# First two column blocks of an input projection: x read transposed, mean squares by a matmul with ones, token half 0 before half 1

## The chip, the cores and the metric

One core of a Trainium2 chip runs the whole kernel. The metric is the device time of one execution in microseconds (us), as the median of several runs. Engines are named as in the profile: PE is the matrix engine, DVE the vector engine, ACT the scalar engine, POOL the GpSimd engine, SP the engine that issues most of the DMAs.

## The reference, cut to what matters

The kernel computes one decoder layer in float32 on 1024 tokens of width 1024. Only its head matters here:

```python
def rms_norm(x, g):
    y = x * lax.rsqrt(jnp.mean(jnp.square(x), axis=-1, keepdims=True) + NORM_EPS)
    return y * g

h = rms_norm(x, in_norm_g)          # 1024 tokens x 1024 features
proj = h @ w_in                     # 1024 x 10240: q,k,v,g | xr,gr | m_ret,m_rnn
...
return rms_norm(x + ..., final_norm_g)
```

## The kernel before

**Products.** All products of the projection have features on the partitions: a weight tile of 128 features by 128 output columns is the stationary operand, and 512 tokens (a token half) move. So the normalised x has to lie with features on partitions, in `actv` (`ax(p, k, half)`: p is HI or LO, k one of 8 feature tiles, half one of 2 token halves). For accuracy each float32 operand is split in a rounded part HI and a rest LO, and each product is three matmuls, HI by HI, HI by LO and LO by HI (`mm3`, L322 to L326). The split is always the same pair of steps: ACT copies with rounding (HI), DVE subtracts (LO).

**The head of the program, lines L549 to L561, L936 to L945, L1319 to L1330, L1873 to L1882.** SP loads x as 8 tiles of 128 tokens by 1024 features (512 KB each), the first weight block (256 columns, slot 0 of `raw`) after the second tile, four small constants after the fourth, and the second weight block (slot 1) after the last. Per tile ACT squares it with a running sum along the free axis and takes the root (L349, L351); DVE takes the reciprocal of one number per partition and multiplies the tile (L356, L358). When four tiles are through, PE turns them by 32 transposes of 128x128 against an identity (L373), ACT copies each turned bank with the scale g to HI (L394), and DVE makes LO (L400). The second four tiles go the same way, their 32 transposes standing inside the product of slot 0 (`first_block`, L377).

**The order of the first two blocks.** `feature_jobs` runs, for one slot, four jobs: token half 0 with two column tiles, then token half 1 with two; slot 0 first, then slot 1. A job is 8 feature tiles by 3 matmuls, so the two blocks are 2 x 4 x 8 x 3 = 192 matmuls. Slot 0 uses PSUM banks 0 to 3, slot 1 banks 4 to 7. ACT applies the sigmoid from PSUM to `ost` (`evac_job`, L1339).

**What comes next.** The other 28 input blocks are done by a seven-product scheme with combined operands (`in_product`, L948). Its activation operands sc1 to sc4 are sums of quarters of the normalised x. In the kernel before these quarters are first put together again from HI and LO by `whole` (L1989, four calls: HI plus LO of 4 feature tiles), then combined (`comb`, L1994), and each result is split (`comb_hi` on ACT, L1369; `comb_lo` on DVE, L1997). The list of these DVE steps stands at L2004 to L2033, in one order with the preparation of the first weights (`combine_t13`, `combine_t2`, `combine_t4`, `prep_lo`). The first of the seven products (q == 0) waits for `prep_lo(0, 0, "b1")`, which in that list stands behind c3f, t13, the LO of sc3, t2, c2f, cbf and the LO of sc2. Engines run their instructions strictly in the order written; semaphores order them between engines, and every order is written out by hand.

**The rest** (the blocks' steady loop, retention, the recurrent unit, the output products, the convolution network) isn't touched but for counts of semaphores.

Of the kernel before, what the change touches and what calls it, by code (L numbers as in the profile page):

```python
# [14 lines left out]
F32 = mybir.dt.float32  # L15
# [93 lines left out]
def build(nc, a):  # L109
# [36 lines left out]
    x_in, _ = at("x_in", [P, KT, D], F32, B)  # L146
    xn_in, _ = at("xn_in", [P, KT, D], F32, B + 32 * K1)
# [30 lines left out]
    def chunk_set(tag, e):  # L178
# [70 lines left out]
    names = """alone const_in cs_in xt0 xt1 xt2 xt3 xt4 xt5 xt6 xt7 raw0 raw1 whi0 whi1 wsp0 wsp1 blk0 blk1 ini  # L249
        ss_done std_done rs_done xn_done tr_ps nhi_done nsp_done  # L250
# [6 lines left out]
        a11_in a12_in a22_in xs_hi xs_lo s3_f s2_f s1_f s4_f  # L257
        fraw0 fraw1 f_t13 f_t2 f_t4 f_hi f_lo f_pr f_u f_c tap0 tap1 conv_done g_silu a_mul h_st2
        dwr0 dwr1 dw_hi dw_lo dh_hi dh_lo d_b d_ps d_add tq_in tq_st tq_out
        out_t out_done""".split()  # L260
# [6 lines left out]
            "g_in": ("cs_in", 32), "d_s": ("rate", 3)}  # L267
# [92 lines left out]
    def turn_bank(n):  # L360

        return n if n < 8 else 4 + n % 4

    def turn_pe(pe, jobs, src, xn_sem, ps_sem, sp_sem):

        for n in jobs:
            half, k = n // 8, n % 8
            if k == 0:
                pe.wait_ge(xn_sem, 4 * half + 4)
            if n >= 8:  # L370
                pe.wait_ge(sp_sem, n - 3)
            for t in range(4):
                last = pe.transpose(ps[:, turn_bank(n), t * P:(t + 1) * P],  # L373
                                    src[:, 4 * half + t, k * P:(k + 1) * P], ident[:, :])
            last.then_inc(ps_sem, 1)

    def first_block(pe, slot_jobs, src_turn, sems):  # L377


        def around(job, k, after):  # L380
            if job == 0 and not after:
                pe.wait_ge(sems[2], k + 1)
            if job == 2 and k == 0 and not after:
                turn_pe(pe, range(8, 12), src_turn, *sems)
            if job == 2 and not after:
                pe.wait_ge(sems[2], 9 + k)
            if job == 2 and k < 4 and after:
                turn_pe(pe, (12 + k,), src_turn, *sems)
        slot_jobs(around)

    def turn_hi(act, n, dst, g, ps_sem, hi_sem):
        half, k = n // 8, n % 8
        act.wait_ge(ps_sem, n + 1)
        act.activation(dst(HI, k, half), ps[:, turn_bank(n), :], ACT.Copy,  # L394
                       scale=prm[:, g + k:g + k + 1]).then_inc(hi_sem, 1)

    def turn_lo(dve, n, dst, g, hi_sem, sp_sem):
        half, k = n // 8, n % 8
        dve.wait_ge(hi_sem, n + 1)
        dve.scalar_tensor_tensor(out=dst(LO, k, half), in0=ps[:, turn_bank(n), :], scalar=prm[:, g + k:g + k + 1],  # L400
                                 in1=dst(HI, k, half).bitcast(F32), op0=ALU.mult, op1=ALU.subtract).then_inc(sp_sem, 1)

# [6 lines left out]
    FIRST = [True, True, True, False, True, False, False]  # L409
    LAST = [False, True, True, False, False, True, True]  # L410
# [136 lines left out]
    with block:  # L547
# [3 lines left out]
        def _(sp_):  # L551
            x_t = a["x"].rearrange("b (t p) d -> p (b t) d", p=P)
            for t in range(KT):
                sp_.dma_start(x_in[:, t, :], x_t[:, t, :]).then_inc(sem[f"xt{t}"], 16)
                if t == 1:
                    load_columns(sp_, FIRST_PAIR, 0, a["w_in"][0], FIRST_COL)
                if t == 3:
                    for dst, src in ((prm, "prm"), (con, "con"), (ident, "ident"), (mask, "mask")):
                        sp_.dma_start(dst[:, :], a[src]).then_inc(sem["const_in"], 16)
# [2182 lines left out]
```

## Time and profile before

| what | before |
|---|---|
| median of 3 runs | 2028.03 us (2027.58 to 2028.80) |
| profiled execution, first to last instruction (span) | 2026.2 us |
| PE busy | 1987.1 us, 98% |
| DVE busy | 1404.8 us, 69% |
| ACT busy | 905.8 us, 45% |
| granted TensorE clock, mean | 0.999 |

The profile is of one execution; the profiled execution has no time of its own beside its span, so the 1.83 us between the span and the median stand for what lies around the span. "Busy" counts the time in which an engine has an instruction under way, and matmuls overlap: one takes some 0.39 us from start to end, but the next one starts 0.227 us after it.

### The profile page before, as it was taken

How to read it: one execution, taken by the hardware profiler on the slowest of the kernel's cores; microseconds unless marked ns; L12 is line 12 of the kernel's file. 1: busy time of each engine (PE TensorE's matmuls, PEld its weight loads, DVE VectorE, ACT ScalarE, POOL GpSimd, SP SyncE). 2: the span in 40 equal slices, each digit the busy share in tenths (PEclk: the TensorE clock that was granted, in tenths of full speed). 3: DMA queues.
4: the chain of work that ended last, by engine and by line, in shares of the span. 5: the costliest groups of instructions: out<-in, count | busy, mean ns of one | idle time of the engine just before them, and what ended most of it. 6: DMA issues, size and time to landing. Idle time of an engine off the chain costs nothing.

```text
span 2026.2 us, 25232 instructions
## 1 busy us (share of the span) xinstructions
PE 1987.1 (98%) x9332; PEld 1658.1 (82%) x9332; DVE 1404.8 (69%) x1714; ACT 905.8 (45%) x1154; POOL 228.9 (11%) x188
## 2 busy tenths in 40 slices
PE   7999999999999999999999999999999999999998
PEld 6888888888888888887788887898788888888887
DVE  6876876876744444614877877847988788776766
ACT  6443344344445555412444443345544444443335
POOL 0000000000000000001254544300000000000000
PEclk9999999999999999999999999999999999999999
DMA  5334445445444443445334234741222122156633
GB/s 203 125 132 138 154 161 182 154 159 185 164 169 175 156 156 125 146 150 187 99 120 120 78 119 131 264 147 52 94 83 104 62 83 104 62 172 232 209 101 133
DMA packets 184580, 283.01 MB, mean 140 GB/s; under 512 B 9792, under 2 KB 123840, under 8 KB 184256
## 3 DMA queue, kind: packets, MB, share of 16 engines
q1 hardware_dynamic: 164208, 204.52, 30.4%
q0 software_dynamic: 20304, 77.60, 9.8%
q8 instruction: 40, 0.66, 0.1%
q14 instruction: 28, 0.23, 0.0%
HBM read 198.20 MB, written 83.89 MB: 139 GB/s over the span
## 4 chain that ended last, share of the span: by engine, by line
PE 83%; DVE 11%; ACT 2%; issue 2%; DMA 1%; SPq 1%; DVEq 0%; ACTq 0%
PE ps L324 27%; PE ps L326 27%; PE ps L325 27%; DVE wx L1953 1%; DVE ws L307 1%; PE ps L1140 1%; DMA qkv<-scr_v 1%; DVE ost L1901 1%; DMA raw<-w_rnn_o 0%; PE ps L373 0%; DVE stage L2058 0%; ACT ri L1508 0%; DVE th L2142 0%; DVE ri L2153 0%; DVE th L2146 0%
## 5 line engine op out<-in xcount | busy, mean ns | idle before, releaser
L1366 ACT ACTIVATE wx<-raw 128x1024 fp32r<-128x1024 f32 (+1 forms) x152 | 137.4, 906 | 270.5 <-DVE raw L1929 148.3
L324 PE MATMUL ps<-xs,wx 128*128 128x512 f32 x612 | 239.0, 391 | 2.0 <-DVE xs L2381 1.6
L326 PE MATMUL ps<-xs,wx 128*128 128x512 f32 x612 | 238.2, 389 | 0.0
L325 PE MATMUL ps<-xs,wx 128*128 128x512 f32 x612 | 238.1, 389 | 0.0
L1953 DVE TENSOR_TENSOR wx<-raw,wx 128x1024 fp32r<-128x1024 f32 (+1 forms) x152 | 156.3, 1029 | 32.2 <-ACT wx L1366 32.2
L324 PE MATMUL ps<-sc,wx 128*128 128x512 f32 x448 | 174.8, 390 | 1.2 <-ACT ub L1398 1.2
L326 PE MATMUL ps<-sc,wx 128*128 128x512 f32 x448 | 174.3, 389 | 0.0
L325 PE MATMUL ps<-sc,wx 128*128 128x512 f32 x448 | 174.3, 389 | 0.0
L324 PEld LDWEIGHTS ps<-xs,wx 128*128 128x128 f32 x612 | 114.9, 188 | 28.6 <-issue 2.7
L326 PEld LDWEIGHTS ps<-xs,wx 128*128 128x128 f32 x612 | 114.9, 188 | 23.9
L325 PEld LDWEIGHTS ps<-xs,wx 128*128 128x128 f32 x612 | 114.9, 188 | 23.6
L1398 ACT ACTIVATE ub<-ps 128x512 f32<-128x512 f32 x112 | 66.4, 596 | 146.9 <-PE ps L326 144.4
L324 PE MATMUL ps<-actv,wx 128*128 128x512 f32 x336 | 130.7, 389 | 0.0
L325 PE MATMUL ps<-actv,wx 128*128 128x512 f32 x336 | 130.7, 389 | 0.0
L326 PE MATMUL ps<-actv,wx 128*128 128x512 f32 x336 | 130.7, 389 | 0.0
L307 DVE TENSOR_TENSOR ws<-raw,ws 128x2048 fp32r<-128x2048 f32 x32 | 73.3, 2289 | 78.6 <-ACT ws L303 78.6
L324 PE MATMUL ps<-wsd,hsd 128*128 128x512 f32 x308 | 119.9, 389 | 0.0
L325 PE MATMUL ps<-wsd,hsd 128*128 128x512 f32 x308 | 119.8, 389 | 0.0
L326 PE MATMUL ps<-wsd,hsd 128*128 128x512 f32 x308 | 119.8, 389 | 0.0
L303 ACT ACTIVATE ws<-raw 128x2048 fp32r<-128x2048 f32 x32 | 61.2, 1912 | 95.4 <-DMA raw<-w_rnn_o 52.2
L324 PE MATMUL ps<-yh,ws 128*128 128x512 f32 x256 | 100.1, 391 | 0.9 <-DVE yh L2239 0.8
L324 PEld LDWEIGHTS ps<-sc,wx 128*128 128x128 f32 x448 | 84.1, 188 | 20.2 <-ACT ub L1398 2.9
(270 smaller groups left out, 4826.8 us busy)
## 6 DMA issues: line engine op xcount, KB each, us to landing
raw<-w_in SPq DMA_DIRECT2D x80, 512.0 KB, 5.3
scr<-ost POOLq DMA_DIRECT2D x32, 1024.0 KB, 5.3
raw<-w_up SPq DMA_DIRECT2D x44, 512.0 KB, 3.9
tq<-w_down SPq DMA_DIRECT2D x88, 128.0 KB, 3.1
scr_t<-tq POOLq DMA_DIRECT2D x22, 512.0 KB, 3.2
scr_h<-vt POOLq DMA_DIRECT2D x11, 1024.0 KB, 4.3
scr_v<-ost POOLq DMA_DIRECT2D x8, 1024.0 KB, 4.4
qkv<-scr SPq DMA_DIRECT2D x64, 128.0 KB, 3.0
```

The lines of the kernel that those rows point to most:

```text
L303: act.activation(ws[:, slot, HI, 0:n], raw[:, slot, 0:n], ACT.Copy).then_inc(w_hi[slot], 1)
L307: dve.tensor_tensor(ws[:, slot, LO, 0:n], raw[:, slot, 0:n], ws[:, slot, HI, 0:n].bitcast(F32), ALU.subtract).then_inc(w_split[slot], 1)
L324: pe.matmul(out, w(HI), x(HI), start=first, stop=False, skip_group_check=True)
L325: pe.matmul(out, w(HI), x(LO), start=False, stop=False, skip_group_check=True)
L326: return pe.matmul(out, w(LO), x(HI), start=False, stop=last, skip_group_check=True)
L1140: last = pe.transpose(ps[:, 5, m * P:(m + 1) * P], on_of(h, j)[:, slot, m * P:(m + 1) * P], ident[:, :])
L1366: act.activation(dst, src, ACT.Copy).then_inc(sem["f_hi"], 1)
L1398: act.activation(ub[:, which, :], ps[:, 4 * u + BANKS[q], :], ACT.Copy).then_inc(sem["f_u"], 1)
L1901: ins = dve.scalar_tensor_tensor(out=dst, in0=s_, scalar=w, in1=dst, op0=ALU.mult, op1=ALU.add)
L1953: dve.tensor_tensor(dst, src, hi.bitcast(F32), ALU.subtract).then_inc(sem["f_lo"], 1)
```

## The change

The host passes x transposed as well (`xT`, features by tokens). The head loads `xT` instead of x, in 8 pieces of 2 feature tiles by 512 tokens (512 KB each): the four of token half 0, then the first weight block in two halves with semaphores of their own, the four constants, two pieces of half 1, the second weight block, and the last two pieces. There are no transposes. Per half: ACT squares four pieces, DVE adds the tiles pairwise (half 1: further, to one tile), PE multiplies a 128x128 matrix of ones by the sums of squares (plain float32, 512 columns; four matmuls for half 0, one for half 1), which gives the sum over all features of each token on every partition; ACT takes the root of that 128x512 tile, DVE its reciprocal. Then for each feature tile DVE multiplies x by g and by the reciprocal (`token_f`), ACT makes HI and DVE makes LO. The order of the 192 products is half 0 with slot 0, half 0 with slot 1, half 1 with slot 0, half 1 with slot 1. Because the normalised x stays in float32 in `xn_in`, the four calls of `whole` are dropped, and the counts of `q_st` change with them. Semaphores that are used only late in the program share those of the head (`late`).

```diff
@@ allocation
-    x_in, _ = at("x_in", [P, KT, D], F32, B)
-    xn_in, _ = at("xn_in", [P, KT, D], F32, B + 32 * K1)
+    x_in, _ = at("x_in", [P, 2, KT, HALF], F32, B)
+    xn_in, _ = at("xn_in", [P, 2, KT, HALF], F32, B + 32 * K1)
+    ones, e = at("ones", [P, P], F32, C + 16 * K1)
+    std_row, e = at("std_row", [P, 2, HALF], F32, e + 512)
+    rs_row, _ = at("rs_row", [P, 2, HALF], F32, e)
...
@@ SP
-            for t in range(KT):
-                sp_.dma_start(x_in[:, t, :], x_t[:, t, :]).then_inc(sem[f"xt{t}"], 16)
...
+            for n in range(4):
+                load_x(n)
...
+            sp_.dma_start(r[:, 0:4, :], v[:, 0:4, FIRST_COL:FIRST_COL + BC]).then_inc(sem["wa_in"], 16)
+            sp_.sem_inc(raw_in[0], 16)
+            sp_.dma_start(r[:, 4:8, :], v[:, 4:8, FIRST_COL:FIRST_COL + BC]).then_inc(raw_in[0], 16)
...
+            for n in range(4, 6):
+                load_x(n)
             load_columns(sp_, FIRST_PAIR, 1, w_in, FIRST_COL + BC)
+            for n in range(6, 8):
+                load_x(n)
@@ POOL
+            pool.memset(ones[:, :], 1.0).then_inc(sem["ini"], 1)
@@ PE
-            pe.wait_ge(sem["const_in"], 16 * 4)
-            in_sems = (sem["xn_done"], sem["tr_ps"], sem["nsp_done"])
-            turn_pe(pe, range(8), xn_in, *in_sems)
...
+            def square_sums(half, tiles, first_sum):
+                for n, k in enumerate(tiles):
+                    pe.wait_ge(sem["sq_p"], first_sum + n)
+                    h, at_ = xn_at(half, k)
+                    last = pe.matmul(ps[:, 7 - half, :], ones[:, :], xn_in[:, h, at_, :], start=n == 0,
+                                     stop=n == len(tiles) - 1, skip_group_check=True)
+                last.then_inc(sem["ss_ps"], 1)
+            square_sums(0, (0, 2, 4, 6), 1)
+            for half in range(2):
+                for slot in range(2):
+                    w = ws[:, slot, :, :].rearrange("p a (k c) -> p a k c", k=KT)
+                    for k in range(KT):
+                        if half == 0 and slot == 0 and k == 0:
+                            pe.wait_ge(sem["wa_lo"], 1)
+                        if half == 0 and k == (0 if slot else 4):
+                            block_ready(pe, FIRST_PAIR, slot)
+                        if half == 0 and slot == 1 and k == 3:
+                            square_sums(1, (0,), 8)
+                        if slot == 0:
+                            pe.wait_ge(sem["nsp_done"], 8 * half + k + 1)
+                        for m in range(2):
+                            last = mm3(pe, ps[:, 4 * slot + 2 * half + m, :], lambda q: w[:, q, k, m * P:(m + 1) * P],
+                                       lambda q: ax(q, k, half), k == 0, k == KT - 1)
@@ ACT
+            act.activation(rms_rs[:, 0:1], eps_norm, ACT.Sqrt)
...
+            for q in range(4):
+                squares(0, q)
+            act.wait_ge(sem["wa_in"], 16)
+            act.activation(ws[:, 0, HI, 0:BE // 2], raw[:, 0, 0:BE // 2], ACT.Copy).then_inc(sem["wa_hi"], 1)
+            deviations(0)
+            token_hi(0)
...
+            act.activation(ws[:, 0, HI, BE // 2:], raw[:, 0, BE // 2:], ACT.Copy).then_inc(w_hi[0], 1)
+            for n in range(1, 5):
+                token_hi(n)
+            split_hi(act, FIRST_PAIR, 1)
+            for n in range(5, 8):
+                token_hi(n)
+            for q in range(4):
+                squares(1, q)
+            deviations(1)
...
+            for n in range(8, 16):
+                token_hi(n)
+                if n in (11, 13):
+                    evac_job(FIRST_PAIR, 0, (n - 11) // 2, ACT.Sigmoid, 0)
@@ DVE
+            for q in range(4):
+                h, k = xn_at(0, 2 * q)
+                dve.wait_ge(sem["ss_done"], q + 1)
+                dve.tensor_tensor(xn_in[:, h, k, :], xn_in[:, h, k, :], xn_in[:, h, k + 1, :], ALU.add).then_inc(sem["sq_p"], 1)
+            dve.wait_ge(sem["wa_hi"], 1)
+            dve.tensor_tensor(ws[:, 0, LO, 0:BE // 2], raw[:, 0, 0:BE // 2], ws[:, 0, HI, 0:BE // 2].bitcast(F32),
+                              ALU.subtract).then_inc(sem["wa_lo"], 1)
+            def inverse(half):
+                dve.wait_ge(sem["std_done"], half + 1)
+                dve.reciprocal(rs_row[:, half, :], std_row[:, half, :]).then_inc(sem["rs_done"], 1)
+                dve.wait_ge(sem["rs_done"], half + 1)
...
+            inverse(0)
+            dve.wait_ge(sem["const_in"], 16 * 4)
+            for n in range(KT):
+                token_f(n)
+                if n:
+                    token_lo(n - 1)
+                if n == 1:
+                    dve.wait_ge(w_hi[0], 1)
+                    dve.tensor_tensor(ws[:, 0, LO, BE // 2:], raw[:, 0, BE // 2:], ws[:, 0, HI, BE // 2:].bitcast(F32),
+                                      ALU.subtract).then_inc(w_split[0], 1)
+            token_lo(KT - 1)
+            split_lo(dve, FIRST_PAIR, 1)
+            for n, (to, of, size, after) in enumerate(((0, 4, 2, 0), (2, 6, 2, 0), (0, 2, 2, 6), (0, 1, 1, 7))):
+                dve.wait_ge(sem["ss_done"], 8 if n else 7)
+                if after:
+                    dve.wait_ge(sem["sq_p"], after)
+                dve.tensor_tensor(xn_in[:, 1, to:to + size, :], xn_in[:, 1, to:to + size, :], xn_in[:, 1, of:of + size, :],
+                                  ALU.add).then_inc(sem["sq_p"], 1)
+            inverse(1)
+            for n in range(KT, 2 * KT):
+                token_f(n)
+                if n > KT:
+                    token_lo(n - 1)
+            token_lo(2 * KT - 1)
...
-            whole(caf, 0, 0)
-            whole(cbf, 0, 1)
-            step_done(2)
-            comb(c3f, caf, cbf, ALU.subtract)
+            comb(c3f, x11, x21, ALU.subtract)
             combine_t13(0, 0, (raw_in[0], IN_PAIRS[0] * 32 + 32))
+            comb_lo(sc3[:, LO, :, :], c3f, sc3[:, HI, :, :], 1)
+            combine_t2(0, 0, 0)
+            step_done(1)
+            comb(c2f, x22, c3f, ALU.subtract)
             step_done(3)
-            comb_lo(sc3[:, LO, :, :], c3f, sc3[:, HI, :, :], 1)
-            whole(cbf, 4, 1)
-            combine_t2(0, 0, 0)
-            step_done(5)
-            comb(c2f, cbf, c3f, ALU.subtract)
-            step_done(6)
-            comb(cbf, c2f, caf, ALU.add)
+            comb(cbf, x11, c2f, ALU.add)
             comb_lo(sc2[:, LO, :, :], c2f, sc2[:, HI, :, :], 2)
             prep_lo(0, 0, "b1", 1)
             combine_t4(0, 0, 0, 1)
-            step_done(8)
-            whole(caf, 4, 0)
+            comb(caf, x12, c2f, ALU.subtract)
```

## Rows read from the trace of the kernel before

**Rows 1.** The page's part 1, busy time of each engine and its share of the span.

```profile
PE 1987.1 (98%) x9332; PEld 1658.1 (82%) x9332; DVE 1404.8 (69%) x1714; ACT 905.8 (45%) x1154; POOL 228.9 (11%) x188
```

**Rows 2.** Waits of PE, whole run: us in total, times, longest; the two longest.

```profile
PE ps L373 <- DVE xn_in L358: 14.8, 1, 14.8
PE ps L324 <- DVE ktm L2268: 8.1, 11, 1.4
```

**Rows 3.** Timeline, PE, first 40 us: start, us, engine, line, operation, tiles.

```profile
14.76 5.82 PE L373 MATMUL ps<-ident,xn_in 128*128 128x128 f32 x32 [14.76 <-DVE xn_in L358]
20.34 0.47 PE L324 MATMUL ps<-actv,ws 128*128 128x512 f32 x1
...
31.33 1.91 PE L373 MATMUL ps<-ident,xn_in 128*128 128x128 f32 x16
...
33.49 0.50 PE L324 MATMUL ps<-actv,ws 128*128 128x512 f32 x1 [0.26 <-DVE actv L400]
```

**Rows 4.** Timeline, PE: the first of the seven products, and the fourth, 36 matmuls on.

```profile
68.10 0.39 PE L324 MATMUL ps<-actv,wx 128*128 128x512 f32 x1
...
76.26 0.39 PE L324 MATMUL ps<-sc,wx 128*128 128x512 f32 x1
```

**Rows 5.** Windows of the transposes: width, PE busy (count), PEld busy (count), granted clock, DMA.

```profile
14.70:19.20 4.50, 4.44 (x21) 4.47 (x22) 1.00 1.05 393
19.20:20.34 1.14, 1.14 (x13) 1.14 (x11) 1.00 1.09 384
```

**Rows 6.** Chain that ended last, first 20 us: start, us, what.

```profile
2.27 6.34 DMA raw<-w_in
```

**Rows 7.** Timeline, ACT: the first square, and the table load before the first sigmoid.

```profile
4.64 1.06 ACT L349 ACTIVATE xn_in<-x_in 128x1024 f32<-128x1024 f32 x1 [2.18 <-DMA x_in<-x]
...
39.05 1.28 ACT L1342 ACT_TABLE_LOAD   x1
```

**Rows 8.** Groups by line and form, DVE: reciprocals of 1 and 8 elements, a TENSOR_TENSOR of 8 elements.

```profile
L2218 DVE RECIPROCAL hn<-hn 128x1 f32<-128x1 f32 x32 | 4.9, 154 | 2.4 <-ACT hn L1559 2.4
L2117 DVE RECIPROCAL sp<-sp 128x8 f32<-128x8 f32 x1 | 0.2, 203 | 0.0
L2122 DVE TENSOR_TENSOR sp<-sp 128x8 f32<-128x8 f32 x7 | 1.2, 168 | 0.2
```

**Rows 9.** Timeline, DVE: the steps between the normalised x and the first of the seven products.

```profile
46.45 2.29 DVE L1995 TENSOR_TENSOR c3f<-caf,cbf 128x2048 f32<-128x2048 f32 x1
...
50.80 2.29 DVE L1999 TENSOR_TENSOR sc<-c3f,sc 128x2048 fp32r<-128x2048 f32 x1 [0.92 <-ACT sc L1371]
53.01 2.29 DVE L1991 TENSOR_TENSOR cbf<-actv 128x2048 f32<-128x2048 f32 x1
55.21 0.69 DVE L1922 TENSOR_TENSOR raw<-raw,tt 128x512 f32<-128x512 f32 x1
55.81 2.29 DVE L1995 TENSOR_TENSOR c2f<-cbf,c3f 128x2048 f32<-128x2048 f32 x1
...
62.55 1.22 DVE L1953 TENSOR_TENSOR wx<-raw,wx 128x1024 fp32r<-128x1024 f32 x1
63.87 0.69 DVE L1929 TENSOR_TENSOR raw<-raw 128x512 f32<-128x512 f32 x1
```

**Rows 10.** Timeline, DVE: four SCALAR_TENSOR_TENSOR of 512 elements in a row.

```profile
32.69 2.73 DVE L400 SCALAR_TENSOR_TENSOR actv<-ps,prm,actv 128x512 fp32r<-128x512 f32 x4 [4.51 <-ACT actv L394]
```

**Rows 11.** Groups by line and form, ACT: rounding copies of 512 from SBUF and PSUM.

```profile
L1577 ACT ACTIVATE yh<-ych 128x512 fp32r<-128x512 f32 x32 | 20.2, 632 | 20.1 <-DVE ych L2232 20.1
L394 ACT ACTIVATE actv<-ps,prm 128x512 fp32r<-128x512 f32 x16 | 10.4, 689 | 8.1 <-PE ps L373 8.0
```

**Rows 12.** Timeline, DVE: LO of b22, and the first long idle time after them.

```profile
76.57 0.68 DVE L1953 TENSOR_TENSOR wx<-raw,wx 128x512 fp32r<-128x512 f32 x1
...
85.25 0.69 DVE L2058 TENSOR_TENSOR stage<-ub 128x512 f32<-128x512 f32 x1 [2.06 <-ACT ub L1398]
```

**Rows 13.** DMA issues of the first 60 us: KB each, median us to landing.

```profile
scr_a<-actv SPq DMA_DIRECT2D x1, 2048.0 KB, 9.8
```

More of the change, by code:

```diff
@@ L358, in norm_apply_dve @@
         dve.tensor_scalar(dst[:, t, :], src[:, t, :], rms_rs[:, t:t + 1], None, ALU.mult).then_inc(xn_sem, 1)
[L360 to L401, printed above, removed]
     E_B11, E_B21, E_T4, E_T2, E_B22, E_T1, E_T3 = range(7)
@@ L936, in _ @@
                 pe.sem_inc(blk[slot], 1)
[L937 to L945 removed]
+            pe.wait_ge(sem["ini"], 2)
+            def square_sums(half, tiles, first_sum):
[21 more added lines that the diff above has]
+                                       lambda q: ax(q, k, half), k == 0, k == KT - 1)
+                            if k == KT - 1:
+                                last.then_inc(blk[slot] if half == 1 and m == 1 else sem["job"], 1)
             def in_product(b, q, u):
@@ L1328, in _, with squares, deviations @@
-            split_hi(act, 0, 1)
-            for n in range(8, 16):
-                turn_hi(act, n, ax, PRM["in_g"], sem["tr_ps"], sem["nhi_done"])
+            act.activation(rms_rs[:, 0:1], eps_norm, ACT.Sqrt)
+            def squares(half, q):
+                act.wait_ge(sem[f"xt{4 * half + q}"], 16)
+                h, k = xn_at(half, 2 * q)
+                act.activation(xn_in[:, h, k:k + 2, :], x_in[:, half, 2 * q:2 * q + 2, :], ACT.Square).then_inc(sem["ss_done"], 1)
+            def deviations(half):
+                act.wait_ge(sem["ss_ps"], half + 1)
+                act.activation(std_row[:, half, :], ps[:, 7 - half, :], ACT.Sqrt, scale=1.0 / D,
+                               bias=eps_norm).then_inc(sem["std_done"], 1)
@@ new lines, in token_hi @@
+            def token_hi(n):
+                half, k = n // KT, n % KT
+                h, at_ = xn_at(half, k)
+                act.wait_ge(sem["xn_done"], n + 1)
+                act.activation(ax(HI, k, half), xn_in[:, h, at_, :], ACT.Copy).then_inc(sem["nhi_done"], 1)
+            for q in range(4):
[3 more added lines that the diff above has]
+            deviations(0)
@@ L1340, in evac_job @@
                 half, m = job // 2, job % 2
-                job_wait(i, slot, job)
+                if i == FIRST_PAIR and job < 3:
+                    act.wait_ge(sem["job"], FIRST_JOBS.index((slot, job)) + (0 if (slot, job) == (1, 2) else 1))
+                else:
+                    job_wait(i, slot, job)
                 act.activation(ost[:, slot, m, half * HALF:(half + 1) * HALF], ps[:, 4 * slot + job, :],
@@ L1380, in _ @@
             prep_hi(0, 0, "b1")
-            for job in range(2):
-                evac_job(FIRST_PAIR, 1, job, ACT.Sigmoid, 0)
             act.wait_ge(sem["f_t4"], 1)
@@ L1385, in _ @@
             prep_hi(0, 0, "t2")
-            comb_hi(sc1[:, HI, :, :], cbf, 7)
-            evac_job(FIRST_PAIR, 1, 2, ACT.Sigmoid, 0)
-            evac_job(FIRST_PAIR, 1, 3, ACT.Sigmoid, 0)
+            comb_hi(sc1[:, HI, :, :], cbf, 4)
+            for job in range(2, 4):
+                evac_job(FIRST_PAIR, 1, job, ACT.Sigmoid, 0)
             act.wait_ge(blk[1], IN_PAIRS[0] + 1)
@@ new lines, in _, with token_f @@
+            dve.wait_ge(sem["wa_hi"], 1)
[5 more added lines that the diff above has]
+                dve.wait_ge(sem["rs_done"], half + 1)
+            def token_f(n):
+                half, k = n // KT, n % KT
+                h, at_ = xn_at(half, k)
+                dve.scalar_tensor_tensor(out=xn_in[:, h, at_, :], in0=x_in[:, half, k, :],
+                                         scalar=prm[:, PRM["in_g"] + k:PRM["in_g"] + k + 1], in1=rs_row[:, half, :],
+                                         op0=ALU.mult, op1=ALU.mult).then_inc(sem["xn_done"], 1)
```

134 lines of the change are left out of this document (61 added, 73 removed).

## The prediction

> **What bounds the kernel now.** I read the page's busy times first: PE is busy 98% of the span, the other engines far less [rows 1]. So time can come only from what PE waits for and from what PE does beside products. The list of PE's waits says where it waits: 14.8 us before the first transpose, then 8.1 us in eleven pieces in a later stage that the change doesn't touch [rows 2]. The timeline of the opening shows the rest [rows 3]: transposes from 14.76, the first product at 20.34, and between 31.33 and the end of the two blocks a second set of transposes with a short wait at 33.49. The first of the seven products starts at 68.10 [rows 4]. The 192 products of the two blocks need 192 x 0.2267 = 43.5 us, the pitch being (76.26 - 68.10)/36 [rows 4]; 68.10 - 20.34 = 47.8, so 4.2 us between them is transposes and waiting. Everything after 68.10 hangs on PE, so the change is worth what it moves the start of the first of the seven products. I call that moment Q.
>
> **Part 1, the start for half 0.** ACT's first square starts when the first 512 KB are there, 4.64 [rows 7]; the fourth piece of 512 KB had landed at 2.27 + 6.34 = 8.61 [rows 6]. I take the same times for pieces of xT (2 KB rows between the 4 KB rows of x and the 1 KB rows of w_in, which that row covers), so the fifth piece, the weights, lands near 9.9, before its turn. The squares end at 5.7 and at 9.7; DVE adds in 0.69 [rows 9]. (On DVE the next instruction starts some 0.09 before the last one's end: 0.60 apart for 512 elements, 1.13 for 1024, 2.20 for 2048, and 0.66 for a SCALAR_TENSOR_TENSOR of 512, (2.73 - 0.75)/3 [rows 9, 10].)
>
> The plain float32 matmul with ones isn't in the trace. Below: one pass, 0.23. Above: `mm3` computes three of the four HI/LO combinations in three pitches, the fourth makes 4 x 0.2267 = 0.91. I take 0.91, since the f32 transposes, which only pass a value on, already take more than their share: 128 columns in 1.14/11 = 0.10 against 0.057 for a quarter of 0.2267 [rows 5]. The Trainium skill (FP8 and Floating Point Precision, TensorE Precision Notes) gives four passes for true FP32, the same sum; no row here shows such a matmul.
>
> Pace: the first 21 transposes, after 14.7 us of idleness, came 0.214 us apart, the next ones 0.10 [rows 5]. The granted clock stands at 1.00 in both rows, yet the ratio is that of 1.2 to 2.4 GHz and lasts 4.4 us. So I cost PE at half pace for its first 4.4 us. Sums start at 6.5, 8.3, 10.1 and, with the pace rising at 10.9, 11.4; the last ends at 12.3, with drain 12.4. The root from PSUM takes 0.69 [rows 11]: 13.1.
>
> **The reciprocal** is the term that decides. One of 512 elements isn't there. One element takes 154 ns, eight take 203; an ordinary operation of eight takes 168 [rows 8]. Slope: 49/7 = 7.0 ns an element; or (203 - 168)/7 = 5.0 more than the ordinary one's 1.07 (2.20/2048 from [rows 9]), that is 6.1. I take 6.4, nearer the second, which compares equal sizes: 0.15 + 511 x 0.0064 = 3.4 us. Ends: 0.69, as any 512 elements, if eight elements say nothing of many, and 4.4 above (see the third rival).
>
> It ends at 16.6. Then token_f 0.75, ACT's HI 0.63, token_f of the next tile beside it, LO 0.69 [rows 9, 10, 11]: first product at **18.8** instead of 20.34, though 32 transposes are gone. PE has been idle for over 6 us, so half pace again: six products 2.6, to 21.4. DVE puts the second half of the weights' LO (1.13) between: LO of tile 1 comes at 21.5. Tile 1 runs slow until 23.2, ends at 23.7; six more tiles at 1.36 make 31.9, faster than DVE's 0.66 + 0.60 = 1.26 a tile needs PE to wait for. Slot 1 follows: its split ends near 31.5, its raw load landed long before. 48 x 0.2267 + 0.91 for the sum of half 1: 43.7. Half 1 is 96 x 0.2267 = 21.8: PE would be ready for Q at **65.5**, 2.6 us earlier than before, by PE's own work.
>
> **Part 2, DVE's list for half 1.** The sum stands at slot 1's fourth tile, 31.9 + 4.1 = 36.0. The four adds (3 x 1.13 + 0.69, behind the split that ends at 31.5) end at 35.8, just in time. Sum to 37.1, root 37.8, reciprocal 41.2, token_f to 42.0. Then seventeen steps in turn, 0.66 + 8 x 1.26: last LO at 52.0, and 0.4 for ACT, which has a table load of 1.28 [rows 7] and two sigmoids between tiles 11 and 14: 52.4. Now the old list runs: before, from the start of c3f to the end of b1's LO was 63.77 - 46.45 = 17.3, of which 2.2 was a `whole` [rows 9], so 15.1. Q = **67.6**. The chain on DVE is 2.1 longer than PE's own; PE waits at Q for b1's LO.
>
> So `whole` saves four times 2.2 us of DVE, three of them ahead of Q, and PE is rid of the 4.2 us of half 1's transposes and wait, but the two reciprocals put 6.8 us back on the one chain, and half 1's float32 work (16 steps) stands behind the second.
>
> **What is free, and its cover.** Scratch store of a quarter of half 1 (wait for 12 LOs): issued near 49 instead of 43, 9.8 to land [rows 13]: 59, needed after 65. The sigmoids' stores through POOL's queue leave up to 15 us later, their buffers are next written some 20 us on. The constants land some 2 us later, needed at 16.6. The memset of ones lies under the loads. SP issues the same 16 DMAs. After Q: LO of t4 comes about 3.1 us after Q, used at Q + 5.4; b22 at about Q + 11, used at Q + 16.3. LO of b22 began at 76.57 before [rows 12] and begins near 78.2 now; DVE was idle 2.06 us before 85.25 [rows 12], which takes that up. The 64 transposes and 5 sums otherwise leave no trace. So I carry the shift of Q to the end unchanged.
>
> **Sum.** 67.6 - 68.10 = -0.5 us against a span of 2026.2, 2025.7; the median stands 1.83 above the span: **2027.5 us**. Measurement tells 0.2%, 4.1 us, from no change.
>
> **Rivals.**
> 1. *The reciprocal is an ordinary operation* (0.69). Both terms lose 2.8. Then the chain is at 67.6 - 5.5 = 62.1, PE's own work at 65.5 - 2.8 = 62.7 decides: -5.4, 2022.6. For it: nothing wide was seen. Against: eight elements cost more than an ordinary eight. 0.12.
> 2. *The sums are one pass each* (0.23). The last ends 1.2 earlier, the second sum 0.7: 65.7, 2025.6. 0.10.
> 3. *DVE's chain costs more than it saves*: the reciprocal takes eight elementary steps an element. 8 x 1.07 x 512 = 4.4 us, twice 1.0 more: Q at 69.6, PE waiting 3 us for b1's LO, 2029.5, slower. From 3.7 us a reciprocal on, Q passes 68.10; only from 5.7 us would it be over 0.2%. Against: the slopes of 6.1 to 7.0. The Trainium skill (VectorE: DVE Perf Modes, First, the fixed hardware budget) describes the reciprocal as an iterative divide with a repeat count of 8, which would be this case; no wide reciprocal is in the trace of before. 0.14.
>
> The forecast has what is left, 0.64.
>
> Range: forecast's own 2025.5 to 2028.7 (reciprocal 3.2 to 3.7, sums 0.23 to 0.91, loads 0.5 us either way, 0.6 of run spread); with rivals 2 and 3 it is 2024.2 to 2029.8; rival 1 stays outside. Faster by over 0.2%: 0.13; within: 0.84; slower: 0.03 (a reciprocal near 6 us, or a late load on top).
>
> **What would show it.** RECIPROCAL of 128x512 near 3.4 us, twice, PE idle during the first; first product near 18.8, with the first pitches near 0.43; PE waiting some 2 us at the first `actv,wx` product, released by b1's LO on DVE, near 67.6; no later wait of PE that wasn't there. Wrong if that product starts before 64 or after 70, if PE waits within half 1, or if waits grow later while Q moved early.

## The result, and the profile after

| what | before | after |
|---|---|---|
| median | 2027.85 us (2026.91 to 2029.49, 20 runs) | 2030.59 us (2028.94 to 2033.33, 20 runs) |
| ratio | | 1.0014, 95% interval 1.0008 to 1.0020 |
| profiled execution, span | 2026.2 us | 2029.0 us |
| PE busy | 1987.1 us | 1988.1 us |

The change costs 2.7 us, a loss of 0.14%: smaller than the 0.2% that the prediction called the least to be told, yet outside its range. First the totals of the changed kernel and the list of what PE waits for, to be read beside [rows 1, 2].

```profile
PE 1988.1 (98%) x9278; PEld 1652.2 (81%) x9278; DVE 1410.4 (70%) x1721; ACT 902.2 (44%) x1141; POOL 225.5 (11%) x189
```

```profile
PE ps L332 <- DVE ktm L2328: 8.1, 11, 1.4
PE ps L921 <- DVE xn_in L1906: 6.7, 1, 6.7
PE ps L332 <- DVE actv L1930: 6.4, 1, 6.4
...
PE ps L332 <- DVE wx L2025: 1.9, 1, 1.9
PE ps L332 <- ACT ub L1427: 1.8, 4, 0.8
...
PE ps L332 <- DVE yacc L2312: 1.3, 1, 1.3
PE ps L332 <- DVE ws L315: 1.3, 1, 1.3
...
PE ps L332 <- DVE mix L2393: 0.6, 1, 0.6
```

The 14.8 us before the first transpose have become 6.7 and 6.4, before and behind the sums of squares, with PE's 6.67 us for the sums between them. Two entries are as foreseen: the wait at `wx` (Q, the start of the first of the seven products) and the one at `actv`. Three are not: 0.8 us at once for ACT's `ub` (before, no wait for it was over 0.3), and, in a stage 1200 us behind the change, 1.3 us for `yacc` and 1.3 us for DVE's split of the weights of `w_out` (`ws`). One wait of that stage has shrunk, `mix` from 1.7 to 0.6. The timeline gives the places; PE first.

```profile
6.65 6.67 PE L921 MATMUL ps<-xn_in,ones 128*128 128x512 f32 x8 [6.65 <-DVE xn_in L1906]
19.75 0.77 PE L332 MATMUL ps<-actv,ws 128*128 128x512 f32 x1 [6.43 <-DVE actv L1930]
20.31 0.63 PE L333 MATMUL ps<-actv,ws 128*128 128x512 f32 x1
20.74 0.63 PE L334 MATMUL ps<-actv,ws 128*128 128x512 f32 x1
...
66.19 0.39 PE L334 MATMUL ps<-actv,ws 128*128 128x512 f32 x1
68.45 0.47 PE L332 MATMUL ps<-actv,wx 128*128 128x512 f32 x1 [1.87 <-DVE wx L2025]
...
84.63 0.39 PE L334 MATMUL ps<-sc,wx 128*128 128x512 f32 x1
85.85 0.47 PE L332 MATMUL ps<-sc,wx 128*128 128x512 f32 x1 [0.83 <-ACT ub L1427]
```

The sums end at 13.3, the first product starts at 19.75 with matmuls 0.43 apart, the blocks end at 66.42 (the last start and one pitch) and Q is at 68.45, 0.35 later than in [rows 4]. At 85.85, where the seventh of the seven products begins, PE has lost another 1.0 us: the pitch before it is 1.22 instead of 0.227. Nothing like it is in the trace of before. Now DVE and ACT around these places.

```profile
14.07 3.35 DVE L1914 RECIPROCAL rs_row<-std_row 128x512 f32<-128x512 f32 x1 [0.81 <-ACT std_row L1327]
...
38.62 3.35 DVE L1914 RECIPROCAL rs_row<-std_row 128x512 f32<-128x512 f32 x1 [1.94 <-ACT std_row L1327]
...
64.88 2.28 DVE L2066 TENSOR_TENSOR sc<-c2f,sc 128x2048 fp32r<-128x2048 f32 x1
67.08 1.22 DVE L2025 TENSOR_TENSOR wx<-raw,wx 128x1024 fp32r<-128x1024 f32 x1
...
82.55 1.22 DVE L2025 TENSOR_TENSOR wx<-raw,wx 128x1024 fp32r<-128x1024 f32 x1
83.87 0.69 DVE L2001 TENSOR_TENSOR raw<-raw 128x512 f32<-128x512 f32 x1
```

```profile
84.59 0.63 ACT L1392 ACTIVATE wx<-raw 128x512 fp32r<-128x512 f32 x1 [4.38 <-DVE raw L2001]
85.13 1.06 ACT L1427 ACTIVATE ub<-ps 128x512 f32<-128x512 f32 x2
```

Both reciprocals take 3.35 us, and b1's LO (67.08) ends just before Q: the chain of the prediction. The second place is read backwards from PE's 85.85. The product there was released by ACT's copy `ub` at 85.13. That copy needs only PSUM, but ACT had been idle for 4.38 us, standing in its order at the HI copy of block 1's t4, which waits for DVE's t4 (L2001), started at 83.87. So DVE's list, which the prediction left at Q, decides PE's time once more, 17 us later.

Six profiles show how much of this is the kernel's and how much the execution's: of the unchanged kernel, beside the one shown, two more (and one with an unused input, below), of the changed one three in all.

| | first product | Q | shift at 100 us | span |
|---|---|---|---|---|
| before, 3 profiles | 20.34, 19.92, 21.20 | 68.10, 67.67, 68.94 | 0, -0.43, +0.81 | 2026.2, 2026.1, 2026.8 |
| after, 3 profiles | 19.75, 19.51, 18.94 | 68.45, 68.21, 68.34 | +1.30, +1.03, +1.92 | 2029.0, 2028.7, 2029.4 |

(The shift is that of PE's same matmul against the first profile of before.) On the average Q is 0.1 later, PE's matmuls near 100 us are 1.3 later, and the end is 2.7 later. The third profile after is of experiment 12, whose computation and order are those of the changed kernel.

### The profile page after: what moved, and what is told of

Read it like the earlier page. It is cut to its first block, busy times and chain, and to the rows that moved or that the text cites. A ratio compares the mean times of both kernels' runs of the same rounds, so it can differ in the third digit from the quotient of the medians.

```text
span 2029.0 us, 25120 instructions
## 1 busy us (share of the span) xinstructions
PE 1988.1 (98%) x9278; PEld 1652.2 (81%) x9278; DVE 1410.4 (70%) x1721; ACT 902.2 (44%) x1141; POOL 225.5 (11%) x189
## 4 chain that ended last, share of the span: by engine, by line
PE 78%; DVE 13%; issue 4%; ACT 3%; POOL 1%; DMA 1%; SPq 0%; DVEq 0%; POOLq 0%; ACTq 0%
PE ps L332 26%; PE ps L334 25%; PE ps L333 25%; DVE wx L2025 1%; DVE ws L315 1%; POOL msg L894 1%; PE ps L1137 1%; DVE ost L1975 1%; DMA qkv<-scr_v 0%; DVE tt L1987 0%; PE ps L921 0%; DVE stage L2118 0%; ACT ri L1537 0%; DVE th L2202 0%; DVE ri L2213 0%
## 5 line engine op out<-in xcount | busy, mean ns | idle before, releaser
L315 DVE TENSOR_TENSOR ws<-raw,ws 128x2048 fp32r<-128x2048 f32 x31 | 72.0, 2324 | 78.0 <-ACT ws L311 78.0
```

What stands on the lines that cost most here:

```text
L315: dve.tensor_tensor(ws[:, slot, LO, 0:n], raw[:, slot, 0:n], ws[:, slot, HI, 0:n].bitcast(F32), ALU.subtract).then_inc(w_split[slot], 1)
```

## The experiments

Differences are of medians, to the kernel before on the same chip, whose median there was 2028.82 (experiments 1 to 4), 2028.23 (5 to 8), 2028.29 (9, 10), 2028.37 (11) and 2027.88 us (12). Each interval is some 1.8 us to either side, so differences of 1 us are read from the profiles and only supported by the medians. A wait of PE is given as the time lost against its pitch of 0.227; the idle time in the profile's rows is some 0.16 shorter.

The theories: the loss is DVE's list, bound until some 100 us, through the wait at Q and the one at the seventh product; or it is the one wait at Q; or PE's clock, which a long wait lets fall; or something late and unconnected.

**1. b1's LO earlier.** DVE's `prep_lo` of b1 goes up to stand right behind the LO of sc3. On ACT (not shown) b1's HI goes up too, and the HI of sc2 goes behind two sigmoids.

```diff
             comb_lo(sc3[:, LO, :, :], c3f, sc3[:, HI, :, :], 1)
+            prep_lo(0, 0, "b1", 1)
             combine_t2(0, 0, 0)
...
             comb_lo(sc2[:, LO, :, :], c2f, sc2[:, HI, :, :], 2)
-            prep_lo(0, 0, "b1", 1)
```

> Only the place of the first weights' split is changed: on ACT and DVE the HI and LO of b1 stand right behind those of sc3, ahead of c2f, cbf and the split of sc2. Nothing is left out. Theory A (DVE's list is the bound, in two places: at the first of the seven products by b1's LO, and again before the seventh by the U copy that ACT makes only after DVE's t4 of block 1): the first of the seven products starts near 66.4 instead of 68.45, when PE's own work is done, but t4's LO then holds the third product by about 0.4, and the seventh product still starts near 85.8, because DVE's list is as long as before; total within 0.3 us of the changed kernel. Rival B (the wait at the first product is the loss and the rest is independent of it): the seventh product starts 2.0 earlier and the kernel is 2.0 us faster than the changed one.

2030.91 us, +2.1 (ratio 1.0011, 1.0002 to 1.0020). The wait at Q is gone, Q at 66.19:

```profile
65.97 0.39 PE L334 MATMUL ps<-actv,ws 128*128 128x512 f32 x1
66.19 0.39 PE L332 MATMUL ps<-actv,wx 128*128 128x512 f32 x1
```

and the list of PE's waits has it at the other place, longer:

```profile
PE ps L332 <- ACT ub L1427: 3.0, 4, 2.1
```

Two us gained at Q, of which 1.3 were lost again before the seventh product (the expectation had all of it lost). So the wait at Q alone is not the cause; DVE's list behind it is.

**2. The copy ahead of the wait.** ACT copies the first block's sixth partial result out of PSUM before it waits for block 1's t4.

```diff
+                        in_copy(b, u, U_P5)
...
-                in_copy(b, u, U_P5)
+                if b:
+                    in_copy(b, u, U_P5)
```

> Only ACT's order in the first of the seven-product blocks is changed: the copy of the fifth product (U_P5) stands ahead of the wait for DVE's t4 of block 1. Nothing is left out. Theory A: the wait of 1.0 us before the seventh product goes, its start moves from 85.85 to about 84.85, the first product stays at 68.45; 1.0 us faster than the changed kernel. Rival B (the wait was for something else, the split of b22 or the fourth operand on DVE): the seventh product stays at 85.85.

2031.24 us, +2.4 (1.0011, 1.0002 to 1.0020). No wait at the seventh product, and no gain. This profile alone doesn't show that the edit removed the wait, since PE was itself late here; 1 against 3 does. PE at Q, and its windows there (width, PE busy, granted clock, DMA share, GB/s):

```profile
68.26 0.66 PE L332 MATMUL ps<-actv,wx 128*128 128x512 f32 x1 [1.87 <-DVE wx L2027]
68.72 0.63 PE L333 MATMUL ps<-actv,wx 128*128 128x512 f32 x1
69.15 0.63 PE L334 MATMUL ps<-actv,wx 128*128 128x512 f32 x1
```

```profile
68.26:71.71 3.45, 3.45 (x9) 0.52 0.99 330
71.71:76.00 4.29, 4.29 (x20) 0.99 0.26 106
```

Behind the same wait of 2.0 us the granted clock stood at 0.52, that is 1.2 GHz, and eight matmuls came 0.427 apart instead of 0.227: 1.6 us. In the profile shown after, the same stretch was at full pace. So the wait at Q has a second price, which only some executions pay.

**3. Both edits of 1 and 2.**

> Both edits of e1_b1_first and e2_copy_first. Theory A: first product near 66.4, seventh near 83.2, 2.6 us faster than the changed kernel, so together they are worth more than the 0 and the 1.0 of each alone. Rival B (the two waits add): 3.0 us. If the late part of the loss (about 1.4 us that the profile shows between 1282 and 1302 us in the changed kernel) comes from the change, it is in this kernel too, and the kernel is about level with the one before; if it is the spread of one execution, this kernel is 1.2 us faster than the one before.

2029.52 us, +0.7 (1.0005, 0.9996 to 1.0014), 2.0 to 2.5 us faster than the changed kernel (whose own differences are +2.7 in the first result and +3.2 in 5) where 2.6 were expected. Block 0's seventh product, which waited 2.1 us in 1, waits no more. The wait has moved on by one block, to block 1's seventh product:

```profile
99.54 0.39 PE L334 MATMUL ps<-sc,wx 128*128 128x512 f32 x1
101.67 0.50 PE L332 MATMUL ps<-sc,wx 128*128 128x512 f32 x1 [1.74 <-ACT ub L1427]
```

**4. Without the cost of both reciprocals.** The inverse of the root is left out: the normalised x of the two blocks and the operands is multiplied by the root itself.

```diff
-                dve.reciprocal(rs_row[:, half, :], std_row[:, half, :])
+                dve.tensor_scalar(rs_row[:, half, :], std_row[:, half, :], 1.0, None, ALU.mult)
```

> The two reciprocals of 512 elements are replaced by multiplications by 1.0, so x is scaled by the deviation and not by its inverse; the rest is the changed kernel. Theory A (each reciprocal is about 2.8 longer than an ordinary operation, the first delays PE's start, the second DVE's list): first product of the two blocks near 17.0 instead of 19.75, the first of the seven near 63.7 (PE's own work), no wait before the seventh, 5.8 us faster than the changed kernel. Rival B (only the first reciprocal is on the path, because the wait at the seven products has another cause): a rigid shift of 2.8 us with both later waits left, 2.8 us faster.

2023.99 us, -4.8 (0.9977, 0.9968 to 0.9986). First product 16.02, Q 63.18 with no wait, no long wait at the seventh product. At 100 us it is 6.1 us ahead of the changed kernel; the instruction that took the reciprocal's place takes 0.43, so 2 x 2.92 = 5.8 us were taken out. All of both reciprocals lies on the path. By the medians the kernel is 7.5 to 8.0 us faster than the changed one; the 2 us beyond 5.8 are within what two intervals of 1.8 allow, and part of them can be the clock at Q, which this kernel doesn't pay.

**5. The changed kernel again**, as a mate for 6 to 8.

> The changed kernel once more, unaltered, for a second profile. Theory C (the wait of 2.0 us at the first of the seven products lets PE's clock fall in some executions, so that they lose up to 1.7 us more): either a profile like the first, with 0.227 us between matmuls behind that wait, or one with 0.427 for the next eight, as in the profile of e2_copy_first. Theory D (the 1.4 us lost between 1282 and 1302 us in the first profile come from the change): the loss is there again. If D is wrong it is anywhere between 0 and 1.5, as it was in the four other kernels (0.0 to 1.1).

2031.46 us, +3.2 (1.0014, 1.0005 to 1.0023). Waits as after: 2.0 at Q, 1.0 at the seventh product, 1.1 near 1300 us.

**6. The wait at Q filled** with eight matmuls whose result nobody uses; Q itself doesn't move.

```diff
+            pe.wait_ge(sem["evac"], 1)
+            for n in range(8):
+                pe.matmul(ps[:, 0, :], ax(HI, n, 0, slice(0, P)), ax(HI, n, 0), start=True, stop=True, skip_group_check=True)
```

> Eight extra matmuls (1.8 us) are put on PE between the two blocks and the first of the seven products, into a bank that is overwritten right after, so that PE works through most of its wait for b1's LO. Theory C: the first of the seven products stays near 68.4 and the wait before it shrinks to 0.2; its clock can't fall there, and the median over the executions comes down from that of the changed kernel by 0.3 to 1.0 us (1.7 times the share of the executions in which it fell). Rival (the fall of the clock has no part in the median): the same median as a1_again. If PE, and not DVE, were the bound at that point, the kernel would be 1.8 us slower.

2029.64 us, +1.4 (1.0008, 0.9999 to 1.0017). PE does 1.97 us of useless work:

```profile
66.01 1.97 PE L986 MATMUL ps<-actv 128*128 128x512 f32 x8
68.04 0.47 PE L332 MATMUL ps<-actv,wx 128*128 128x512 f32 x1
```

Q is at 68.04 against 68.21 and the seventh product still waits, yet the median is 1.8 (the mean 1.2) below that of 5. That is more than expected (0.3 to 1.0), within the intervals' reach, and the two profiled executions don't show it (spans 2029.0 and 2028.7). What the rows show is 1.6 us in the two executions whose clock fell (here in 2, and in 12), two of the five profiles with this wait: an estimate of 0.6 us on the average. That it is more is not shown.

**7 and 8. One reciprocal each**, replaced as in 4 (the inverse is left out for token half 1, then for half 0).

> Only the second reciprocal is replaced by a multiplication by 1.0 (token half 1 is scaled by the deviation, not its inverse); the first stays. Theory A: PE starts at 19.5 as before, DVE's list is 2.8 shorter: first of the seven products at PE's own 66.3, no wait left before the seventh (f_t4 of block 1 comes at 81.8), 3.0 us faster than a1_again. Rival B (only the first reciprocal counts): no change.

> Only the first reciprocal is replaced (token half 0). Theory A: everything on PE and on DVE's list moves 2.8 us earlier, PE starts at 16.8, and both waits stay as they are, 2.0 and 1.0; 2.8 us faster than a1_again. With r2_norec_half1 that makes the 5.8 of r1_norec_both. Rival (the start of PE isn't on the path, since DVE's list is the bound): half of the gain or less.

2027.05 us, -1.2 (0.9994, 0.9985 to 1.0003), and 2028.08 us, -0.15 (0.9998, 0.9989 to 1.0007), 4.4 and 3.4 us below 5. At 100 us the profiles are 3.4 and 3.1 us ahead of that of 5, where 2.9 were taken out (0.6 of the 3.4 is that PE started and finished the two blocks earlier in that execution): each reciprocal is paid in full. Without the first, everything moves as a block, and both waits stay (2.0 and 0.95). Without the second, DVE's list is ahead of PE, and there is no wait at Q (65.61) and 0.3 at the seventh product.

**9. A narrow reciprocal.** The sums go to tokens on partitions, 128x4; root and reciprocal are taken there, and four transposes of a broadcast column spread the result over all partitions, in PSUM.

```diff
-                    last = pe.matmul(ps[:, 7 - half, :], ones[:, :], xn_in[:, h, at_, :], start=n == 0,
+                    for c in range(4):
+                        last = pe.matmul(ps[:, 7, c:c + 1], xn_in[:, h, at_, c * P:(c + 1) * P], ones[:, 0:1],
...
+                for c in range(4):
+                    last = pe.transpose(ps[:, 6, c * P:(c + 1) * P],
+                                        rs_row[:, half, c:c + 1].to_broadcast([P, P]), ident[:, :])
...
-                dve.reciprocal(rs_row[:, half, :], std_row[:, half, :])
+                dve.reciprocal(rs_row[:, half, 0:4], std_row[:, half, 0:4])
```

> The mean squares of a half are taken with the tokens on the partitions: per chunk of 128 tokens a matmul with the squares as stationary operand and one column of ones moving, so that root and reciprocal are of 128x4 and not of 128x512; then four f32 transposes of the reciprocal, repeated along the free axis, against the identity put it on all partitions in PSUM, where token_f reads it. Nothing is left out. Theory A (the wide reciprocals cost it): PE's first product near 17.1 instead of 19.5, first of the seven near 64.2, no wait before the seventh; some 5 us faster than the changed kernel, 2 to 3 faster than the one before. Rival (the small f32 matmuls cost what the reciprocal did, since each loads 128 columns of stationary operand four times at the slow pace): first product not before 18.5 and at most 2 us faster than the changed kernel.

2026.45 us, -1.8 (0.9992, 0.9983 to 1.0001), 4.6 to 5.1 us faster than the changed kernel, as expected. First product 17.89 and Q 65.00, each some 0.8 later than expected, no wait at Q.

**10. The same with both edits of 1 and 2.**

> f1_spread with the two edits of e3_both. Theory A: PE is the bound at the first seven products already in f1, so that the order is worth at most 0.3 to 0.8 us more here (the waits before the seventh products of the first two blocks).

2025.19 us, -3.1 (0.9985, 0.9976 to 0.9994): the lowest median of the kernels that compute the whole layer, and the only one of them that is faster than the kernel before by more than its interval. It is 1.3 us below 9 (0.3 to 0.8 expected), which is within the intervals. PE, DVE and ACT at the head of its profile:

```profile
6.71 6.96 PE L922 MATMUL ps<-ones,xn_in 128*128 128x1 f32 x32 [6.71 <-DVE xn_in L1921]
14.24 1.11 PE L931 MATMUL ps<-ident,rs_row 128*128 128x128 f32 x4 [0.57 <-DVE rs_row L1929]
17.68 0.76 PE L332 MATMUL ps<-actv,ws 128*128 128x512 f32 x1 [2.32 <-DVE actv L1945]
```

```profile
14.00 0.18 DVE L1929 RECIPROCAL rs_row<-std_row 128x4 f32<-128x4 f32 x1 [1.02 <-ACT std_row L1340]
```

```profile
13.71 0.27 ACT L1340 ACTIVATE std_row<-ps,sp 128x4 f32<-128x4 f32 x1 [1.98 <-PE ps L922]
```

0.27 + 0.18 + 1.11 stand for 0.69 + 3.35. Q is at 64.70, and of the waits only 0.5 us at block 1's seventh product is left, which the kernel before has too.

**The late microsecond.** Between 1280 and 1322 us the three profiles after lose another 1.3 to 1.6 us against the first of before; the other two of before lose 0.7 and 0.4. Three theories: being later costs by itself, spread, or something of the changed head.

**11. A pure delay** of the kernel before, by 8 and by 16 matmuls ahead of Q (the edit of 6), and its second and third profile, unchanged.

> The kernel before, with eight more matmuls (their result unused) ahead of the first of the seven products: 8 x 0.2267 = 1.81 us on PE. PE's wait of 0.47 near 101 us takes that much up, so everything behind it is 1.34 us later, the shift that the changed kernel has there. If the 1.4 us that the changed kernel loses between 1280 and 1322 us comes from being later by that much (a meeting of transfers and products that depends on the moment), this kernel loses them too: + 2.7 us against the kernel before. If it comes from something in the changed head itself, or is spread between executions, this one is + 1.3 us.

> The same with sixteen matmuls, 3.63 us: + 3.2 us if a delay at the head is carried to the end unchanged, as the prediction took it; over 4.2 us if the late stretch adds its own to any delay.

> The kernel before, unaltered, for a second profile, because all profiles are compared with one of it. Theory D (the changed kernel loses 1.4 us between 1282 and 1322 us by itself): PE's waits over 0.5 or so in that stretch sum to 2.1 again. If it is the spread of one execution, they sum to anything from 2.1 to 3.8, as in the nine other profiles.

> The kernel before, unchanged, a third profile: its waits of PE between 1270 and 1325 us say how far these vary between executions of one kernel. The two profiles so far have 2.1 and 2.5 us, the two of the changed kernel 3.6 and 3.3. Near 2.1 to 2.5 again if the difference belongs to the change, over 3 if it is spread.

1.81 us of work cost +1.6 (1.0008, 0.9999 to 1.0017), 3.63 us cost +3.9 (1.0019, 1.0010 to 1.0028). The wait of 0.47 near 101 us did not take them up: in both profiles it has its old size, and stands as much later as Q. So by the medians a delay at Q is carried to the end as it is, to within the interval of 1.8, and being later is not what makes PE wait for `ws`: that wait is 0 and 0.2 here. The single profiles are less even. From 200 us to the end the one with 8 matmuls gains 0.8 on the first of before and the one with 16 loses 1.3, so spread is of that size. The unchanged kernel's two profiles (single times 2027.75 and 2028.50 us) have no wait for `ws` there either.

**12. The place of the tensors.** xT as an unused input of the kernel before, and xT as the last input of the changed kernel.

> The kernel before, with the 4 MB of xT as one more input that nothing reads. None of the five profiles with the old head has a wait of PE over 0.2 us for the weights of w_out near 1300 us, all eleven with the new head have one of 0.3 to 1.9 us. If the cause is where the tensors lie in memory (xT moves the constants behind it), this kernel shows the wait, near 1 us, and its median is about 1 us above the kernel before. If the cause is in the head's instructions, it has no such wait and equals the kernel before.

> The changed kernel with xT declared as the last input. If it is the place of the tensors that xT moved, the wait for the weights of w_out near 1300 us goes below 0.3 and the median falls by about 1 us, to + 1.7 us against the kernel before; if not, + 2.7 us with a wait near 1.2.

2028.39 us, +0.5 (1.0003, 0.9993 to 1.0013), without the wait; 2031.24 us, +3.4 (1.0016, 1.0006 to 1.0026), with it:

```profile
PE ps L332 <- DVE ws L315: 0.7, 1, 0.7
```

So it isn't the tensors' place. By its profile this kernel also paid the clock at Q: seven pitches from 69.22 on were 0.43.

**What the late rows show.** The lines `ws` in the list of waits don't all mean `w_out`: L315 is a helper's line. At the product of `w_out` (near 1311) ten of the twelve profiles with the new head wait 0.3 to 1.3 us; those of experiments 2 and 10 don't, and their entries of 0.9 and 1.4 are of another product 400 us earlier. The six profiles with the old head have at most 0.2. And it isn't the load of `w_out` that is late. Followed back in the changed kernel:

```profile
1313.14 0.39 PE L332 MATMUL ps<-ws,mix 128*128 128x256 f32 x1 [1.30 <-DVE ws L315]
```

```profile
1300.21 1.81 DVE L2387 TENSOR_TENSOR mxf<-msg,mrb 128x512 f32<-128x512 f32 x1 [3.17 <-POOL msg L894]
...
1310.81 2.29 DVE L315 TENSOR_TENSOR ws<-raw,ws 128x2048 fp32r<-128x2048 f32 x1
```

```profile
1308.80 1.90 ACT L311 ACTIVATE ws<-raw 128x2048 fp32r<-128x2048 f32 x1
```

ACT begins the copy without idle time, so the weights were there; it stood behind the steps for `mix`. Those had waited 3.17 us for POOL (1.19 before), and POOL for a load of `mrb`. SP issued that load behind the 2 MB load of x, and that one 2.3 us later than before: 1.3 is the shift of the whole kernel, the rest is lost around 1281. There DVE and POOL start an instruction within 0.2 us of each other. Before:

```profile
1279.74 2.28 DVE L307 TENSOR_TENSOR ws<-raw,ws 128x2048 fp32r<-128x2048 f32 x1
```

```profile
1279.78 3.39 POOL L917 TENSOR_TENSOR msg<-msg,yacc 128x512 f32<-128x512 f32 x1 [1.11 <-DMA mrb<-scr_r]
```

After:

```profile
1280.98 3.37 DVE L315 TENSOR_TENSOR ws<-raw,ws 128x2048 fp32r<-128x2048 f32 x1
```

```profile
1280.81 1.39 POOL L894 TENSOR_TENSOR msg<-msg,yacc 128x512 f32<-128x512 f32 x1 [0.91 <-DMA mrb<-scr_r]
```

The one that starts first takes its usual time (2.28 for DVE's, 1.3 to 1.4 for POOL's), the other takes 1.1 us (DVE) or 2.1 us (POOL) longer. DVE's split is 1.1 longer after, `yacc` behind it is late, and PE waits for it. In all six profiles with the old head, and in those of experiments 2, 6 and 10, DVE starts first, by 0.03 to 0.41 us; PE then waits at most 0.5 for `yacc`, and the stretch from 1280 to 1322 costs 0.3 us on the average against the first of before. In eight with the new head POOL starts first, by 0.02 to 0.51; PE waits 1.1 to 1.6 for `yacc`, and the stretch costs 0.8 to 1.9, on the average 1.2. (In experiment 4's the two don't meet at the split, but DVE met POOL in the steps before it; it loses 1.1.) This is read from eighteen traces and no run isolates it. Why POOL comes first so often with the new head was not found; the sharing of semaphores (`late`), for one, was not tried by itself.

## Why the prediction was wrong

**The bound at Q and its mechanism** held. PE waits 2.0 us at Q (foreseen 2.1), released by b1's LO, there is no wait over 0.5 us within half 1, and RECIPROCAL of 128x512 is 3.35 twice (taken: 3.4, of ends 0.69 and 4.4). This settles what the rivals took for the reciprocal: it is neither an ordinary operation, nor eight steps an element. The Trainium skill (VectorE: DVE Perf Modes, First, the fixed hardware budget) gives it a repeat count of 8; the third rival's estimate from that, eight elementary steps an element, is 4.4 us. The trace has 3.35, and the measurement decides. Experiments 4, 7 and 8 show that both reciprocals lie on the path. The third rival's time, 2029.5, is nearer to the measured 2030.6 than the forecast is, but by luck: its Q is 1.15 too late, and it has nothing behind Q.

**Q itself was mis-sized** by 0.85, 68.45 for 67.6, and the term is PE's pace in the opening. The sum let half pace end at 10.9, after 4.4 us, as in the kernel before, and the sums of squares at 12.4. They end at 13.3:

```profile
8.49 1.92 PE L921 MATMUL ps<-xn_in,ones 128*128 128x512 f32 x2
...
11.97 0.91 PE L921 MATMUL ps<-xn_in,ones 128*128 128x512 f32 x1
12.72 0.59 PE L921 MATMUL ps<-xn_in,ones 128*128 128x512 f32 x1
```

Each of the four sums stands in the trace as two records. The second sum's start at 8.49 and 9.34, the third's at 10.20 and 11.12, the fourth's at 11.97 and 12.72. So a sum takes 10.20 - 8.49 = 1.71, which is four passes of 0.427, and not one (the second rival). The third started at 10.20 as foreseen (10.1), although ACT had waited 1.09 for its piece of xT, since PE was busy with the second until then. It then ran at half pace to its end at 11.97, and the fourth in part, where the prediction had 11.4 and full pace: that is the 0.9. (The granted clock reads 1.00 in this stretch too, as in [rows 5]; the pace shows in the starts alone.) The delay went through root, reciprocal and first product (19.75 for 18.8) into DVE's list, which took what was foreseen: 11.3 us from the second reciprocal's end to the last LO (11.2, though the prediction's "seventeen steps" behind 42.0 don't add up to its 52.0; they do from 41.2), and 15.0 (15.1) from there to the end of b1's LO. So the term "-0.5" was +0.35 in the profile, and +0.1 on the average of three.

**The step that failed** is "DVE was idle 2.06 us before 85.25 [rows 12], which takes that up", and with it "So I carry the shift of Q to the end unchanged". The idle time is there, but it stands behind the step that matters, DVE's t4 of block 1. Before, DVE began t4 at 81.10, and ACT, in its order, made the copy behind it:

```profile
82.37 0.58 ACT L1398 ACTIVATE ub<-ps 128x512 f32<-128x512 f32 x1
```

It ended at 82.95 for a product that started at 84.42, with 1.5 us to spare. After, t4 began at 83.87, 2.8 us later, and the copy that PE needed at 84.86 held it up until 85.85. Idle time of DVE further down its list could not give that back. Experiments 1 and 3 show it: an edit that removes one of these waits brings the next, because DVE's list is the bound until about 100 us. This is 1.0 us in two profiles of three. The prediction's own sign, "no later wait of PE that wasn't there", is the one that failed.

**Two costs had no term.** The wait at Q was priced by its length. In two of the five profiles that have this wait (experiments 2 and 12) it let the clock fall, 1.6 us more; the prediction used just this effect for the opening, after idleness of over 6 us, and did not ask it of 2 us. Where the clock falls, the wait at the seventh product vanishes (experiment 12), as PE is late itself, so the two prices don't add up. And the late microsecond was behind "isn't touched but for counts of semaphores".

**The account** of 2.7 us, by the means of three profiles each: +0.1 at Q (foreseen -0.5), +1.2 between Q and 100 us, +1.4 from there to the end. From 200 us to the end the six profiles with the old head lie between -0.8 and +1.3 against the first of before (mean 0.1), the twelve with the new head between +0.4 and +2.1 (mean 1.4). Shown: the first two. The third is there beyond the spread; its path is read from the traces, and its cause in the new head is open. That the order of halves or the dropped `whole` cost anything, no run suggests; experiment 10 keeps both and wins 3.1 us.

## What to carry to other kernels

A reciprocal is paid by the elements of its free axis (3.35 us for 512, 0.18 for 4), so it belongs where the numbers lie across partitions, before they are spread and not after. When an edit makes another engine's list the bound, follow that list past the first wait, through every in-order queue that stands behind one of its results, until its lateness is used up; an idle time in the old trace is slack only for what stands behind it on that engine, so ask of each result when it was ready and when it was needed. A short wait of PE may cost most of its length again through the clock (1.6 us after 2.0). A difference far behind the change may come from which of two engines starts first, by a few tenths of a microsecond; look at several profiles before you explain it.

## What the runs showed of the hardware that was not expected

- RECIPROCAL on DVE: 3.35 us for 128x512, 0.18 for 128x4, so (3.35 - 0.18)/508 = 6.2 ns an element, where the ordinary multiply by a constant of the same size took 0.43.
- That multiply (TENSOR_SCALAR, f32, 128x512, 0.43 us) is faster than a TENSOR_TENSOR of the size, 0.69.
- After 2.0 us of waiting PE's matmuls went on at full pace in three profiles, and at a granted clock of 0.52 and 0.50 (1.2 GHz) for eight and seven matmuls in two.
- A plain float32 matmul stands in the trace as two records. Sixteen of one moving column took 6.96 us (32 records, 0.213 apart at half pace), the four sums of 512 columns 6.67.
- A TENSOR_TENSOR of DVE and one of POOL that start within 0.2 us of each other don't run side by side: the first to start keeps its time, the second takes 3.37 for 2.28 (DVE) or 3.39 for 1.3 (POOL).
